# Inverse sums on the diagonal of the matrix that turns the attention probabilities, in place of a pass over their rows

## The reference

```python
def mla_attention(q_nope, q_rope, k_nope, k_rope, v, mask):
    s = (jnp.einsum('bqhd,bkhd->bhqk', q_nope, k_nope)
         + jnp.einsum('bqhd,bkd->bhqk', q_rope, k_rope)).astype(jnp.float32) * MLA_SCALE
    if mask is not None:
        s = jnp.where(mask[None, None], s, NEG)
    p = jax.nn.softmax(s, axis=-1)
    return jnp.einsum('bhqk,bkhd->bqhd', p.astype(v.dtype), v)

def sink_attention(q, k, v, sink, mask):
    ...
    m = jnp.maximum(jnp.max(s, axis=-1, keepdims=True), sk)
    p = jnp.exp(s - m)
    p = p / (jnp.sum(p, axis=-1, keepdims=True) + jnp.exp(sk - m))
    return jnp.einsum('bnhgqk,bnkhd->bnqhgd', p.astype(v.dtype), v)
```

## Time and profile before

| | |
|---|---|
| median of 3 runs | 1419.98 us (1419.6 to 1421.56) |
| the profiled execution | 1421.66 us, span of its instructions 1419.9 us |
| TensorE busy | 1301.4 us, 92% of the span |
| VectorE busy | 625.7 us, 44% |
| ScalarE busy | 425.1 us, 30% |
| attention stage, layer 0 | about 396 to 617 us |
| attention stage, layer 1 | about 1075 to 1290 us |

### The profile page before, as it was taken

The page is one execution under the profiler, slowest core; times in us unless marked ns, Lnnn a source line. Parts: engine busy times, 40 slices in busy tenths (PEclk is TensorE's granted clock), DMA queues, the critical chain, the costliest instruction groups (busy, mean ns, idle before and its releaser), DMA issues.

```text
span 1419.9 us, 18238 instructions
## 1 busy us (share of the span) xinstructions
PE 1301.4 (92%) x7392; PEld 1112.5 (78%) x7392; DVE 625.7 (44%) x1100; ACT 425.1 (30%) x785; POOL 63.1 (4%) x51
## 2 busy tenths in 40 slices
PE   5799999999988889979999999999999887997997
PEld 4699998999744565579989999899984455557997
DVE  3842313354444565353384231244544465635224
ACT  4422311221423432241243231122242334324111
POOL 1100010000000000002120001000000000000211
PEclk9899989999976999979999998999996699997998
DMA  9711010112321223354121111011131210205102
GB/s 351 272 64 59 30 43 31 31 38 71 99 67 67 89 62 95 126 188 147 45 93 63 46 43 43 30 30 31 31 117 67 96 60 0 75 1 202 36 30 104
DMA packets 71518, 112.72 MB, mean 79 GB/s; under 512 B 3329, under 2 KB 55425, under 8 KB 70162
## 3 DMA queue, kind: packets, MB, share of 16 engines
q1 hardware_dynamic: 71442, 111.67, 23.2%
HBM read 94.32 MB, written 16.42 MB: 78 GB/s over the span
## 4 chain that ended last, share of the span: by engine, by line
PE 82%; DVE 8%; ACT 4%; issue 4%; DMA 1%; SPq 1%; DVEq 0%; POOLq 0%; POOL 0%; ACTq 0%
PE psum L938 52%; PE psum L1274 5%; PE psum L1211 4%; PE psum L1245 2%; PE psum L1153 2%; PE psum L1265 1%; PE psum L1201 1%; DVE h_lo L1741 1%; DVE smax L1955 1%; PE psum L1200 1%; PE psum L1289 1%; DMA modw<-in_w_mod 1%; PE psum L1144 1%; DVE scaled L1717 1%; PE psum L1061 1%
## 5 line engine op out<-in xcount | busy, mean ns | idle before, releaser
L938 PE MATMUL psum<-h_hi,w_hi 128*128 128x384 f32 x1440 | 493.8, 343 | 12.1 <-DVE h_lo L1732 9.0
L938 PE MATMUL psum<-h_hi,w_lo 128*128 128x384 f32 x1440 | 487.4, 338 | 0.0
L938 PE MATMUL psum<-h_lo,w_hi 128*128 128x384 f32 x1440 | 486.8, 338 | 0.0
L938 PEld LDWEIGHTS psum<-h_hi,w_hi 128*128 128x128 f32 x1440 | 275.2, 191 | 17.1 <-issue 14.3
L938 PEld LDWEIGHTS psum<-h_hi,w_lo 128*128 128x128 f32 x1440 | 275.5, 191 | 0.0
L938 PEld LDWEIGHTS psum<-h_lo,w_hi 128*128 128x128 f32 x1440 | 275.1, 191 | 0.0
L1777 DVE TENSOR_TENSOR w_lo<-raw,w_hi 128x1024 fp32r<-128x1024 f32 x62 | 77.1, 1244 | 265.8 <-ACT w_hi L1411 265.2
L1411 ACT ACTIVATE w_hi<-raw 128x1024 fp32r<-128x1024 f32 x62 | 65.7, 1060 | 289.9 <-PE psum L938 216.7
L1955 DVE TENSOR_REDUCE smax<-psum 128x1 f32<-128x640 f32 (+7 forms) x80 | 61.7, 771 | 128.7 <-PE psum L1212 90.3
L1274 PE MATMUL psum<-pT,ckv 128*128 128x512 f32 x144 | 78.4, 630 | 15.7 <-DVE pT L1780 15.5
L1583 ACT ACTIVATE pT<-psum 128x512 f32<-128x512 f32 x54 | 32.2, 597 | 133.6 <-issue 60.3
(11 more groups left out here) (216 smaller groups left out, 1486.5 us busy)
## 6 DMA issues: line engine op xcount, KB each, us to landing
raw<-in_w_in SPq DMA_DIRECT2D x18, 1024.0 KB, 5.4
raw<-in_w_mod SPq DMA_DIRECT2D x15, 1024.0 KB, 5.2
x<-xT_scratch SPq DMA_DIRECT2D x4, 2304.0 KB, 11.6
modw<-in_w_mod SPq DMA_DIRECT2D x8, 1024.0 KB, 15.0
raw<-in_w_out SPq DMA_DIRECT2D x10, 768.0 KB, 5.3
tab<-in_c_rope SPq DMA_DIRECT2D x6, 1152.0 KB, 6.9
tok<-in_x_prompt SPq DMA_DIRECT2D x2, 2048.0 KB, 10.0
ckvT_c<-in_cache_mla_ckvT SPq DMA_DIRECT2D x8, 512.0 KB, 4.2
```

Of the source, the lines that this page charges most:

```text
L938: mm = pe.matmul(psum[:, bank, 0:BLK], w_[:, k, :], h[:, k, blk(n)], start=(k == 0 and i == 0), stop=(k == KD - 1 and i == 2))
```

## The change

Each slot of probabilities gets a 128x128 matrix beside it (`diag`, or `diag_s` for the samples' latent attention). The multiplication on VectorE writes the identity times the row's inverse sum, so a diagonal of inverse sums, and the probabilities stay as the exponentials left them. The turn is a product with that diagonal and no longer a transposition with the identity: column q of the result is the turned row q times its inverse sum. The prompt's banded attention (line 1074) stays as it is.

```diff
+    diag = [at(f"diag{s}", SPL_AT + 12288 + 512 * s, [P, P]) for s in range(SLOTS)]
+    diag_s = [at(f"diag_s{i}", a, [P, P]) for i, a in enumerate((ZT_AT + 4096, ZT_AT + 8704))]
...
+    def inverse(j):
+
+        g = GROUP_OF[j]
+        return diag_s[g["idx"] % 2] if g["kind"] == "mla_s" else diag[slot_of(j)]
+
...
                     if g["kind"] == "mla_s":
                         for k in range(4) if i else (4,):
-                            mm = pe.transpose(out[:, tile(k % 4)], probs(g["jobs"][0])[:, tile(k)], ident[:])
+                            mm = pe.matmul(out[:, tile(k % 4)], probs(g["jobs"][0])[:, tile(k)], inverse(g["jobs"][0])[:],
+                                           start=True, stop=True)
                     else:
                         for h in range(HEADS):
-                            mm = pe.transpose(out[:, tile(h)], probs(g["jobs"][h])[:, tile(i)], ident[:])
+                            mm = pe.matmul(out[:, tile(h)], probs(g["jobs"][h])[:, tile(i)], inverse(g["jobs"][h])[:],
+                                           start=True, stop=True)
                     mm.then_inc(pt_T.sem, 1)
...
                     lane.link(dve.reciprocal(rinv[0:rows, s, 0:nh], total))
-                    ts(p_view(j)[:, 0, :], p_view(j)[:, 0, :], rinv[0:rows, s, 0:1], None, ALU.mult, sig=p_ok)
+                    ts(inverse(j)[:], ident[:], rinv[0:rows, s, 0:1], None, ALU.mult, sig=p_ok)
```

## The result

The changed kernel took 1447.13 us (median of 4, 1446.46 to 1451.22) against 1420.06 us: 27.1 us more, a ratio of 1.0195 (95% interval 1.0174 to 1.0215). The prediction was 1453 us, range 1438 to 1464. The profiled execution took 1446.46 us, with a span of 1444.7 us.

The account below looks back on a forecast made before the run. TensorE, in its own queue's order, was taken to bound the attention. Full-clock turns 22.4, half-clock turns 8.5 and hidden turns 4.4, less 2.1 for row passes, gave +33.2 us: 1453 us, range 1438 to 1464.

Parts of the forecast that it names:

- What bounds the kernel: Latent and samples' attention, both layers: TensorE's queue sets the end; stages about 17 us longer each, passed on one for one.
- a sign against it: TensorE's waits: the prediction is wrong if they shrink by more than about 10 us in sum.
- Two records for a tile, at equal pitch: Turns at lines 1245 and 1242: two records instead of one, 0.111 us each at full clock, about 0.213 at half.
- How many tiles are felt: Both attentions: 242 of 368 turned tiles on the chain, 40 more hidden under "issue", 86 at nothing; 35.3 us.
- The turns ahead of the stacked queries: Five places in each layer, four tiles each, hidden by the chain but on the path: 4.4 us.
- The pairs ahead of a block's first weighting: Two batches before a group's first weighting: grow 0.89 us together, under most waits for VectorE's copy; costed at nothing.
- The pass over the rows: VectorE: eighty passes 19.3 us shorter, only four at each layer's start on the path; 2.1 us won.
- The clock: Rival, four low-clock stretches: products instead of transpositions raise the clock earlier, 18 us or half; 1435 or 1444 us; chance 0.14.
- all turns felt: Rival, both attentions: the waits covering 86 tiles depend on them; +42.8 us, 1463 us; chance 0.15.
- nothing felt: Rival, both attentions: TensorE's idle time takes the second records and VectorE's saving comes off; 1401 to 1418 us; chance 0.03.
- one record for a tile: Rival, the turn: product with the diagonal stays one record, only the 2.1 us felt; 1418 us; chance 0.03.
- four times the cost: Rival, the turn: product takes four times the transposition, as the skill's table says; +104 us, 1524 us; chance 0.01.

Follow-up runs that it names:

- e11: Changed kernel with e10's order: the diagonals of heads 0 to 2 of the samples' banded attention written among the maxima; 1449.94 against 1418.68 us, ratio 1.0218.
- e10: Kernel before, row passes of the samples' banded attention's heads 0 to 2 moved behind the maxima two jobs on; 1413.22 against 1420.24 us, ratio 0.9952.
- e3: Changed kernel with the transposition put back, the diagonal written but not used; 1413.96 against 1419.9 us, ratio 0.9966.
- e2: Kernel before with every transposition of the turn issued twice to the same place; 1445.14 us, ratio 1.0191.
- e1: Kernel before with every turn a plain product with the identity, the pass over the rows kept; 1448.57 against 1419.9 us, ratio 1.0214.

## Why the prediction was right or wrong

- **What bounds the kernel**: right. From the end of the attention of layer 0 to the last latent query of layer 1 it is 449.5 us, and 452.6 before; the 3.1 us are the clock's (17 us of low clock there, and 26 before). What was lost in the attention came out at the end. The two stages, for which about 17 us each were expected, became longer by 16.2 and 12.0. TensorE's idle time in the windows of the two stages fell from 61.2 to 52.0 us, by about 9, just under the 10 that the prediction had named as a sign against it.
- **Two records for a tile, at equal pitch**: right. 656 + 80 records at 0.112 us. The factor of four of the Trainium skill's table ("TensorE: Matmul & The Clock Gate", Terms) is a factor of two here: four transpositions 0.44 us, four products 0.90.
- **How many tiles are felt**: right in sum. e11 against e10 gives 36.7 us for 35.3 predicted, and steps at the same level, with the 2.1 us of the passes put back, give 36 to 37 for the changed kernel. The parts are less exact than the sum. A batch behind scores costs 0.51 us more and not 0.44, and at the half clock 0.96 and not 0.85. The turns ahead of the stacked queries, which the chain had hidden under "issue", are felt: lag grows by 0.50 us with each (513.17 in the ledger). The pairs ahead of a block's first weighting are hidden in blocks 3 and 4, where TensorE's wait was 2.6 us and more, and felt from block 5 on (0.50 and 0.46 us at 525 and 527 us).
- **The pass over the rows**: 2.1 us, right: 1.06 us in layer 0 in the ledger, 1.04 in each layer in e3. VectorE's other 17 us bought nothing that the lags show.
- **The clock**: the term that was wrong. I had it at nothing in the sum and as a rival at 0.14. It is worth about 6 us in the medians (33 us at equal mean clock, 27 as measured) and 9.2 in the two profiles. The place was only partly that of the rival. The long low stretches at the heads of the attention hardly changed (17 and 21 us in layer 0 after, 17 and 24 before), and 2.9 of the 9.2 us are there; 2.7 are the dips in blocks 3 and 4 of layer 1, and 3.4 lie between the attentions, where no turn was changed. And the mechanism that I had named, products count and transpositions don't, fell with e2. Why the changed kernel is usually granted more clock stays open; e1 and e2, with as many records, are granted more too.
- **Which execution the sum is made against**: the profile I worked from had a clock of 0.931, and the kernel's own spread with the clock is 12 us (1412.5 to 1424.2). The three executions shown with it (1419.6 to 1421.56) did not tell of that. Counted from 1414 us, the kernel before at a clock of 0.940, the sum of 33.2 gives 1447, which is what the changed kernel took at 0.939 to 0.941. That is found afterwards; the forecast of 1453 was 6 us too high, and it was within its range because the range was wider than that.
- **The rivals**: all turns felt (44.9 us for them, 1463) and nothing felt (1401 to 1418) were both excluded by the lags; one record for a tile and four times the cost by the groups and the pitch.

## What to carry to other kernels

Replacing a float32 transposition by a float32 product doubles TensorE's records and time for it, so folding a scaling into it pays only where TensorE has time to spare; here it bought 2 us of VectorE's path for some 36 of TensorE's. A serial row of passes on which TensorE waits can in part be moved beside its earlier work; here that brought 1.35 us in each layer and cost nothing that the lags show. And a kernel whose TensorE clock comes and goes should be read from two or more profiles, with the granted clock beside each time, before a term of a few us is believed. Sorting the steps between two profiles by the clock level tells the change's own cost from the clock's.

## What the runs showed of the hardware

- In rows of turns at the 2.4 GHz level a float32 product with 128 moving columns takes 0.224 us as two records, a float32 transposition 0.110 as one, a product in the rounded type 0.11 as one, and a transposition in the rounded type 0.086.
- The same program took 1412.5 to 1424.2 us, and the time goes with the mean granted clock (0.941 to 0.929). Dips stood at other places in e10 and e11, where the head of a stage was 1 us shorter, but one also moved by 25 us between two executions of the unchanged kernel (541 and 516 us), so no shift is shown to move them.
- Turns in the rounded type came with less granted clock: 0.912 to 0.929 as products, 0.920 to 0.933 as transpositions, 0.934 to 0.938 as float32 transpositions at otherwise the same load. In seven of the eleven executions with rounded products the time was about 17 us longer. The cause is open.
